# The remainder of a weight unit in the second expert product: one VectorE instruction of 1024 columns in place of two of 512

## The chip, the cores and the metric

One core of a Trainium2 chip runs the whole layer as one program. The metric is device time in microseconds (us), from the start to the end of the program; the median of the runs counts.

## What is computed

The reference is one layer of a diffusion backbone on 256 latent tokens of width 2048: modulated norm, two kinds of attention, an output projection, a second norm, and then product-key experts. Only the last part matters here. Each token picks 16 experts for each of 8 heads out of 16384, and what it adds is a weighted sum of rows of the table `v` (16384 x 2048):

```
act = jax.nn.gelu(jnp.einsum('cd,ced->ce', hc, u[ic]))
wts = (gc * act.astype(jnp.float32)).astype(v.dtype)
return jnp.einsum('ce,ced->cd', wts, v[ic])
```

The kernel computes these products densely for most tokens. For the first product all of `u` is streamed from HBM and multiplied with the activations, and for the second all of `v` is streamed and multiplied with a matrix that holds each token's weight for each expert (zero where it was not picked). The last 64 tokens of the second product are done otherwise: their rows of `v` are gathered by indirect DMA and added up on VectorE. All products are made to nearly fp32 accuracy out of fp32r operands: a value is split into a high part (fp32r) and a remainder (the value less its high part), and the cross products are summed.

## The kernel before

The change lies in the second expert product, the last 580 us or so of the program. The table `v` comes in 256 units of 128 partitions x 1024 fp32 columns (512 KB). Two units are one tile of 128 experts (all 2048 columns), and four units, two tiles, are one block; the value blocks have the numbers 98 to 161. What happens to a unit, in order:

- SyncE's DMA queue (`unit`, L301; later `unit_far`, L413, and `unit_near`, L418) loads it into a slot of a ring in SBUF. Up to block 110 there is one ring of four slots, `raw`; from block 111 on there are two of four, `raw_far` and `raw`, which blocks use in turn. A load into a slot is issued once the remainder of the unit that lay there has been made: it waits for the counter `w_low`, which counts halves.
- ScalarE (`half_high`, L566) rounds it to fp32r, half by half of 512 columns, into `w_hi`. This buffer holds four halves, so a half is rounded once TensorE has done with the half four before it (counter `w_free`). It counts up `w_high` after each half.
- VectorE (`half_low`, L1441, called twice by `split_low`) makes the remainder, unit less `w_hi`, into `w_lo`, which holds four halves too. It waits for `w_high` and counts up `w_low`.
- TensorE (`value_block`, L1378 to L1383) makes five products of 512 columns with a half: three with `w_hi` (L1378, L1379, L1380), for which it waits for `w_high`, and then two with `w_lo` (L1382, L1383), for which it waits for `w_low`. Then it counts up `w_free`.

A tile also has the stationary operand `p_hl`, the weights of the tokens for its 128 experts: ScalarE writes the high part (L870, L871), VectorE the remainder (`p_low`, L2041, 192 columns), and TensorE waits for both at the first of a tile's four halves. `p_hl` has two slots, so ScalarE writes the operand of a tile after TensorE has finished the tile two before.

Instructions of an engine run in program order. VectorE's order is that of `value_turn`: two units (the second tile of a block), `p_low` of the tile that follows, two units (the first tile of the next block), `p_low`. From the fourth turn on each tile also has an `add_half` (L2065, the first two L2072) ahead of `p_low`: 1024 columns of the gathered rows `row_t`, times the weight, are added to `mixed`. In 8 of the 60 turns that have them one more `add_half`, `early`, stands between the first two units. GpSimd fetches the rows of one gather (two indirect DMAs, L526, 128 partitions x 4 KB each) once a slot of `row_t` has been added. Four small `weights` (L2109) and two more stand at the starts of some turns.

Of the kernel before, what the change touches and what calls it, by code (L numbers as in the profile page):

```python
# [21 lines left out]
F32 = mybir.dt.float32  # L22
# [3 lines left out]
ALU = mybir.AluOpType  # L26
# [20 lines left out]
RAW, SPLIT, ADA, ADA1 = 4, 4, 4, 8  # L47
# [49 lines left out]
def block_program(nc, x_lat, x_ctx, par, con, w_ada, stream, sk, x2_dram, out):  # L97
    with ExitStack() as ctx:
# [10 lines left out]
        S = {n: ctx.enter_context(nc.semaphore(n)) for n in sem_names}  # L109
# [13 lines left out]
        def at(name, shape, dt, offset):  # L123
            return nc.alloc_sbuf_tensor_at(name, shape, dt, offset=base + offset)

        raw = at("raw", [P, RAW, UNIT], F32, 0)
        w_hi = at("w_hi", [P, SPLIT, HALF], F32R, 16 * KB)
        w_lo = at("w_lo", [P, SPLIT, HALF], F32R, 24 * KB)
# [101 lines left out]
        early = at("early", [P, 1], F32, R + 160 * KB)  # L230
# [1196 lines left out]
        def _(dve):  # L1427
            V_ = nc.vector
# [8 lines left out]
            def half_low(b, h, ring=raw):  # L1437

                dve.wait_ge(S["w_high"], 8 * b + (h + 1))
                at_ = (h % 2) * HALF  # L1440
                V_.tensor_tensor(w_lo[:, h % SPLIT, :], ring[:, h // 2 % RAW, at_:at_ + HALF],  # L1441
                                 w_hi[:, h % SPLIT, :].bitcast(F32), ALU.subtract).then_inc(S["w_low"], 1)

            def split_low(b, j, ring=raw):
                half_low(b, 2 * j, ring)
                half_low(b, 2 * j + 1, ring)
# [485 lines left out]
            low, high = slice(0, PICKED), slice(PICKED, P)  # L1932
# [84 lines left out]
            b0 = 34 + LATE_ADA_AT  # L2017
# [21 lines left out]
            def p_low(i, s):  # L2039
                dve.wait_ge(S["p_high"], i + 1)  # L2040
                V_.tensor_tensor(p_hl[:, s, DENSE:2 * DENSE], A[:, bass.ds(i, 1), 0:DENSE].rearrange("p a t -> p (a t)"),  # L2041
                                 p_hl[:, s, 0:DENSE].bitcast(F32), ALU.subtract).then_inc(S["p_low"], 1)
# [16 lines left out]
            def mix(r, s, hf):  # L2059

                cols = slice(hf * UNIT, (hf + 1) * UNIT)
                if hf == 0:
                    dve.wait_ge(row_in[s], 32 * r + 32)
                dve.wait_ge(S["mixed"], 8 * r + (2 * s + hf + 1))
                V_.scalar_tensor_tensor(mixed[:, cols], row_t[:, s, cols], weight[:, bass.ds(4 * r + s, 1)],  # L2065
                                        mixed[:, cols], ALU.mult, ALU.add).then_inc(S["mixed"], 1)

            def first_mix(hf):

                cols = slice(hf * UNIT, (hf + 1) * UNIT)  # L2070
                dve.wait_ge(row_in[0], 32)
                V_.tensor_scalar(mixed[:, cols], row_t[:, 0, cols], weight[:, 0:1], None, ALU.mult  # L2072
                                 ).then_inc(S["mixed"], 3 - 2 * hf)

            def ring_of(b):

                return raw_far if b >= FAR_AT and (b - FAR_AT) % 2 == 0 else raw

            def value_turn(b, b0, add=None, early=None):

                split_low(b + (98 + b0), 2, ring_of(98 + b0))
                if early is not None:
                    early()
                split_low(b + (98 + b0), 3, ring_of(98 + b0))
                if add is not None:
                    add(0)
                p_low(2 * b + (2 * b0 + 2), 0)
                split_low(b + (99 + b0), 0, ring_of(99 + b0))
                split_low(b + (99 + b0), 1, ring_of(99 + b0))
                if add is not None:  # L2090
                    add(1)
                p_low(2 * b + (2 * b0 + 3), 1)

            p_low(1, 1)
            gate_tiles(10, 3)
# [1 line left out]
            V_.tensor_tensor(fold[:], ident[:, 0:PICKED], ident[:, PICKED:P], ALU.add)  # L2097
            V_.tensor_scalar(row_far[:], row_near.bitcast(U32), P, None, ALU.add).then_inc(S["far_ready"], 1)
            for b in range(3):
                value_turn(0, b)  # L2100

            dve.wait_ge(S["values_kept"], 32)
            dve.wait_ge(S["p_high_too"], 8)
# [2 lines left out]
            def weights(g):  # L2106
                js = slice(([0] + PICK_ENDS)[g], PICK_ENDS[g])
                dve.wait_ge(pick_in[g], 16 * (js.stop - js.start))
                link(V_.tensor_tensor(weight[:, js], picked[:, js], gate_at[:, js], ALU.mult))  # L2109

            def add_half(n):

                if n < 2:
                    first_mix(n)
                else:
                    mix(n // 8, n // 2 % ROWS, n % 2)

            for g in range(4):
                n = 32 * g
                for b in range(15):  # L2120
                    if b in ((0, 3, 7) if g == 0 else (0,)):
                        weights(g + 2 if g else (b + 1) // 4)
                    three_halves = b in (3, 11)
                    m = n + three_halves
                    value_turn(0, 3 + 15 * g + b, lambda hf: add_half(m + hf), (lambda: add_half(n)) if three_halves else None)
                    n = m + 2
            split_low(161, 2, ring_of(161))
            split_low(161, 3, ring_of(161))

            dve.wait_ge(S["x2_in"], 16)  # L2130

# [155 lines left out]
```

## Time and profile before

| what | value |
|---|---|
| runs | 2033.44, 2037.87, 2039.68 us; median 2037.87 |
| the profiled execution | 2038.55 us; its span 2036.8 us, 1.75 us lie around it |
| TensorE's granted clock | 0.996 of full speed over the span |
| second expert product, first to last product | 1430.8 to 2014.2 us of the span |

The span runs from the first instruction to the last. Rows of a timeline give the start, the length, the engine, the line and the tile; a number behind x says how many instructions are merged, and what stands in brackets is how long the engine sat idle before and what ended it. A matmul shows as 0.39 us, of which the next one overlaps a part.

### The profile page before, as it was taken

To read this page: it belongs to the slowest core of one execution; us is meant where nothing else is said; L and a number is where in the kernel's file an instruction comes from. 1 tells how busy PE (TensorE), PEld (TensorE's weight loads), DVE (VectorE), ACT (ScalarE), POOL (GpSimd) and SP (SyncE) were. 2 spreads that over 40 slices of the span, in tenths; PEclk is the share of its full clock that TensorE was granted. 3 is DMA by queue.
4 is the path that set the end of the run, shared out by engine and by line. 5 is a ranking of instruction groups with operands and counts; after the bars stand their busy time and mean duration, and the time that the engine had idled before them with its cause. 6 is when DMAs were issued, how large, how long until landed. Compare 5 with 4: busy or idle time off the path is not lost.

```text
span 2036.8 us, 35895 instructions
## 1 busy us (share of the span) xinstructions
PE 2002.3 (98%) x10973; PEld 1681.6 (83%) x10973; DVE 1614.8 (79%) x2873; ACT 1117.9 (55%) x2232; POOL 604.2 (30%) x476
## 2 busy tenths in 40 slices
PE   7999999999999999999999999999999999999997
PEld 4578888767999988888888888888878888888886
DVE  4468787897778789899977655676789989989997
ACT  3342225586455555565565555555656666666666
POOL 0000000000000000018888887522455454323320
PEclk9999999999999999999999999999999999999999
DMA  9978887860777655658789887788999999999992
GB/s 387 404 270 295 297 272 288 259 185 2 260 278 273 232 182 179 193 181 192 188 238 282 229 214 189 224 284 284 335 347 379 364 354 356 352 353 367 385 356 97
DMA packets 217706, 550.28 MB, mean 270 GB/s; under 512 B 63888, under 2 KB 89376, under 8 KB 216992
## 3 DMA queue, kind: packets, MB, share of 16 engines
q1 hardware_dynamic: 148688, 465.21, 63.8%
q0 software_dynamic: 52512, 80.00, 15.0%
q10 hardware_dynamic: 16432, 4.19, 1.0%
q8 instruction: 33, 0.54, 0.1%
q14 instruction: 41, 0.34, 0.0%
HBM read 528.11 MB, written 21.07 MB: 270 GB/s over the span
## 4 chain that ended last, share of the span: by engine, by line
PE 90%; DVE 4%; DMA 3%; ACT 1%; issue 1%; DVEq 0%; SPq 0%; ACTq 0%
PE PS L977 23%; PE PS L1338 22%; PE PS L1343 11%; PE PS L1378 6%; PE PS L1383 5%; PE PS L1379 5%; PE PS L1382 5%; PE PS L1380 5%; DMA gt<-grid_scratch 2%; PE PS L1047 1%; DVE st L1649 1%; PE PS L1180 1%; PE PS L964 1%; DMA ada_t<-w_ada 1%; DVE w_lo L1441 1%
## 5 line engine op out<-in xcount | busy, mean ns | idle before, releaser
L566 ACT ACTIVATE w_hi<-raw 128x512 fp32r<-128x512 f32 x1088 | 681.5, 631 | 665.4 <-PE PS L977 255.5
L1441 DVE TENSOR_TENSOR w_lo<-raw,w_hi 128x512 fp32r<-128x512 f32 x1088 | 729.2, 689 | 245.1 <-ACT w_hi L566 211.2
L1338 PE MATMUL PS<-h,w_hi 128*128 128x512 f32 x2048 | 560.4, 395 | 0.0
L1338 PEld LDWEIGHTS PS<-h,w_hi 128*128 128x128 f32 x2048 | 350.7, 189 | 47.1
L1343 PEld LDWEIGHTS PS<-h,w_lo 128*128 128x128 f32 x2048 | 314.3, 189 | 47.9 <-DVE w_lo L1441 4.5
L1343 PE MATMUL PS<-h,w_lo 128*128 128x256 f32 x2048 | 326.7, 281 | 2.7 <-DVE w_lo L1441 2.6
L526 POOL DMA_INDIRECT row_t<-stream,i1T x128 | 163.6, 1278 | 299.2 <-DVE mixed L2065 253.9
L1378 PE MATMUL PS<-w_hi,p_hl 128*128 128x512 f32 x512 | 200.1, 391 | 1.1 <-ACT w_hi L566 0.6
L1382 PE MATMUL PS<-w_lo,p_hl 128*128 128x512 f32 x512 | 199.3, 389 | 0.0
L1379 PE MATMUL PS<-w_hi,p_hl 128*128 128x512 f32 x512 | 199.3, 389 | 0.0
L1380 PE MATMUL PS<-w_hi,p_hl 128*128 128x512 f32 x512 | 199.2, 389 | 0.0
L1383 PE MATMUL PS<-w_lo,p_hl 128*128 128x512 f32 x512 | 199.2, 389 | 0.0
L450 POOL MEMSET acc<- 128x1024 f32 x8 | 7.6, 955 | 595.8 <-PE PS L987 271.3
L566 ACT ACTIVATE w_hi<-raw_far 128x512 fp32r<-128x512 f32 x208 | 131.4, 633 | 82.4 <-PE PS L1383 72.5
L2065 DVE SCALAR_TENSOR_TENSOR mixed<-row_t,gT,mixed 128x1024 f32<-128x1024 f32 x126 | 161.6, 1282 | 0.0
L1441 DVE TENSOR_TENSOR w_lo<-raw_far,w_hi 128x512 fp32r<-128x512 f32 x208 | 137.8, 688 | 20.4 <-ACT w_hi L566 18.2
L1378 PEld LDWEIGHTS PS<-w_hi,p_hl 128*128 128x128 f32 x512 | 96.1, 188 | 24.1 <-issue 2.1
L456 POOL DMA_INDIRECT grid_scratch<-gate_b,addr_b x64 | 110.1, 1720 | 19.5 <-issue 19.5
L977 PE MATMUL PS<-w_hi,hl_h 128*128 128x512 f32 x288 | 113.9, 396 | 1.2 <-DVE w_lo L1441 1.2
L1382 PEld LDWEIGHTS PS<-w_lo,p_hl 128*128 128x128 f32 x512 | 96.1, 188 | 20.6 <-issue 0.4
L1380 PEld LDWEIGHTS PS<-w_hi,p_hl 128*128 128x128 f32 x512 | 96.1, 188 | 20.1
L1383 PEld LDWEIGHTS PS<-w_lo,p_hl 128*128 128x128 f32 x512 | 96.1, 188 | 19.8
(274 smaller groups left out, 3177.7 us busy)
## 6 DMA issues: line engine op xcount, KB each, us to landing
raw<-stream SPq DMA_DIRECT2D x544, 512.0 KB
ada<-w_ada SPq DMA_DIRECT2D x112, 512.0 KB
raw_far<-stream SPq DMA_DIRECT2D x104, 512.0 KB
ada_t<-w_ada SPq DMA_DIRECT2D x64, 512.0 KB, 7.9
grid_scratch<-zeros SPq DMA_DIRECT2D x8, 1536.0 KB, 14.1
gt<-grid_scratch POOLq DMA_DIRECT2D x64, 192.0 KB, 4.6
ada_u<-w_ada SPq DMA_DIRECT2D x16, 512.0 KB
values_scratch<-A ACTq DMA_DIRECT2D x1, 2560.0 KB
```

The costliest lines, as they stand in the source:

```text
L526: nc.gpsimd.indirect_dma_start(row_t[:, j % ROWS, hf * UNIT:(hf + 1) * UNIT], None, rows, bass.IndirectOffsetOnAxis(ap=index[:, j:j + 1], ...
L566: nc.scalar.activation(w_hi[:, (2 * j + hf) % SPLIT, :], ring[:, j, hf * HALF:(hf + 1) * HALF], ACT.Copy).then_inc(S["w_high"], 1)
L977: ins = mm(out_, l_, r_, start=(start and q == 0), stop=(stop and q == 2), skip_group_check=check)
L1338: mm(PS[:, i, :], w_hi[:, h % SPLIT, q * P:(q + 1) * P], h2[:, :, k, :], start=(k == 0), stop=False, skip_group_check=True)
L1343: ins = mm(PS[:, i, 0:T], w_lo[:, h % SPLIT, q * P:(q + 1) * P], h2_h[:, k, :], start=False, stop=(k == KT - 1), skip_group_check=True)
L1378: mm(near_, high, w_hi[:, h % SPLIT, :], start=begin, stop=False, skip_group_check=True)
L1379: mm(near_, low, w_hi[:, h % SPLIT, :], start=False, stop=False, skip_group_check=True)
L1380: mm(far_, both, w_hi[:, h % SPLIT, :], start=begin, stop=False, skip_group_check=True)
L1382: mm(near_, high, w_lo[:, h % SPLIT, :], start=False, stop=end, skip_group_check=True)
L1383: ins = mm(far_, both, w_lo[:, h % SPLIT, :], start=False, stop=end, skip_group_check=True)
L1441: V_.tensor_tensor(w_lo[:, h % SPLIT, :], ring[:, h // 2 % RAW, at_:at_ + HALF], w_hi[:, h % SPLIT, :].bitcast(F32), ALU.subtract).then_in ...
L2065: V_.scalar_tensor_tensor(mixed[:, cols], row_t[:, s, cols], weight[:, bass.ds(4 * r + s, 1)], mixed[:, cols], ALU.mult, ALU.add).then_inc ...
```

## The change

In the value turns VectorE makes the remainder of a whole unit with one instruction of 1024 columns in place of two of 512. A unit's two halves lie side by side in `w_lo` and in `w_hi`. The new `unit_low` waits until both halves of `w_high` are there, and counts up `w_low` by two at its end. `value_turn` loses a parameter that was always 0. All that comes before the second expert product's first two units, and the other engines' code, stay as they were.

```
-            def value_turn(b, b0, add=None, early=None):
-
-                split_low(b + (98 + b0), 2, ring_of(98 + b0))
+            def unit_low(b, j):
+
+                dve.wait_ge(S["w_high"], 8 * b + 2 * j + 2)
+                low, high = (a[:, 2 * j % SPLIT:2 * j % SPLIT + 2, :].rearrange("p a t -> p (a t)") for a in (w_lo, w_hi))
+                V_.tensor_tensor(low, ring_of(b)[:, j, :], high.bitcast(F32), ALU.subtract).then_inc(S["w_low"], 2)
+
+            def value_turn(b0, add=None, early=None):
+
+                unit_low(98 + b0, 2)
                 if early is not None:
                     early()
-                split_low(b + (98 + b0), 3, ring_of(98 + b0))
+                unit_low(98 + b0, 3)
                 if add is not None:
                     add(0)
-                p_low(2 * b + (2 * b0 + 2), 0)
-                split_low(b + (99 + b0), 0, ring_of(99 + b0))
-                split_low(b + (99 + b0), 1, ring_of(99 + b0))
+                p_low(2 * b0 + 2, 0)
+                unit_low(99 + b0, 0)
+                unit_low(99 + b0, 1)
...
-            split_low(161, 2, ring_of(161))
-            split_low(161, 3, ring_of(161))
+            unit_low(161, 2)
+            unit_low(161, 3)
```

On VectorE the first turn with three additions (the seventh value turn) stands so before; `w_lo<-raw,w_hi` is the remainder of halves, `mixed<-...` an `add_half`, `p_hl<-...` the remainder of a tile's operand, `gT<-...` the `weights`:

```order
L2109 TENSOR_TENSOR gT<-i2T,gT 128x4
L1441 TENSOR_TENSOR w_lo<-raw,w_hi 128x512 x2
L2065 SCALAR_TENSOR_TENSOR mixed<-row_t,gT,mixed 128x1024
L1441 TENSOR_TENSOR w_lo<-raw,w_hi 128x512 x2
L2065 SCALAR_TENSOR_TENSOR mixed<-row_t,gT,mixed 128x1024
L2041 TENSOR_TENSOR p_hl<-A,p_hl 128x192
```

and so after the change:

```order
L2115 TENSOR_TENSOR gT<-i2T,gT 128x4
L2083 TENSOR_TENSOR w_lo<-raw,w_hi 128x1024
L2065 SCALAR_TENSOR_TENSOR mixed<-row_t,gT,mixed 128x1024
L2083 TENSOR_TENSOR w_lo<-raw,w_hi 128x1024
L2065 SCALAR_TENSOR_TENSOR mixed<-row_t,gT,mixed 128x1024
L2041 TENSOR_TENSOR p_hl<-A,p_hl 128x192
```

Each pair has become one instruction; nothing has moved past anything. The same holds on VectorE where the additions begin, the fourth and fifth value turns, shown here with the waits, before:

```order
L2109 TENSOR_TENSOR gT<-i2T,gT 128x4 [waits p_low,pick_in0,p_high_too,values_kept]
L1441 TENSOR_TENSOR w_lo<-raw,w_hi 128x512 [waits w_high,dve]
L1441 TENSOR_TENSOR w_lo<-raw,w_hi 128x512 [waits w_high] x3
```

and after:

```order
L2115 TENSOR_TENSOR gT<-i2T,gT 128x4 [waits p_low,pick_in0,p_high_too,values_kept]
L2083 TENSOR_TENSOR w_lo<-raw,w_hi 128x1024 [waits w_high,dve]
L2083 TENSOR_TENSOR w_lo<-raw,w_hi 128x1024 [waits w_high]
L2072 TENSOR_SCALAR mixed<-row_t,gT 128x1024 [waits row_in0]
L2041 TENSOR_TENSOR p_hl<-A,p_hl 128x192 [waits p_high]
```

Four waits for `w_high` have become two, each for a half later than the first of its pair was. TensorE's, ScalarE's and SyncE's instructions are the same in the two kernels.

## Rows read from the trace of the kernel before

**Rows 1.** The page: busy time, DMA share in 40 slices, last chain

```profile
PE 2002.3 (98%) x10973; PEld 1681.6 (83%) x10973; DVE 1614.8 (79%) x2873; ACT 1117.9 (55%) x2232; POOL 604.2 (30%) x476
...
DMA  9978887860777655658789887788999999999992
...
PE 90%; DVE 4%; DMA 3%; ACT 1%; issue 1%; DVEq 0%; SPq 0%; ACTq 0%
```

**Rows 2.** One line's instructions (L1378): count, durations, first and last start

```profile
L1378 PE MATMUL PS<-w_hi,p_hl x512: 389/389/504, 1430.8 to 2013.3; 128*128 128x512 f32 x171
```

**Rows 3.** Waits of TensorE, 1425 to 2014 us: in total, times, longest

```profile
PE PS L1378 <- ACT w_hi L566: 0.6, 1, 0.6
PE PS L1378 <- DVE p_hl L2041: 0.4, 2, 0.2
```

**Rows 4.** Groups by line, 1450 to 2010 us: busy us, mean ns, idle before

```profile
L1441 DVE TENSOR_TENSOR w_lo<-raw,w_hi 128x512 fp32r<-128x512 f32 x285 | 187.7, 688 | 39.3 <-ACT w_hi L566 28.4 <-issue 8.8
...
L566 ACT ACTIVATE w_hi<-raw 128x512 fp32r<-128x512 f32 x284 | 177.2, 631 | 121.5 <-PE PS L1383 92.3 <-DMA raw<-stream 14.7 <-issue 8.7
L2065 DVE SCALAR_TENSOR_TENSOR mixed<-row_t,gT,mixed 128x1024 f32<-128x1024 f32 x126 | 161.6, 1282 | 0.0
...
L2041 DVE TENSOR_TENSOR p_hl<-A,p_hl 128x192 fp32r<-128x192 f32 x123 | 43.2, 352 | 0.0
```

**Rows 5.** Timeline of a tile in the steady part, three engines

```profile
1803.85 0.63 ACT L566 ACTIVATE w_hi<-raw_far 128x512 fp32r<-128x512 f32 x1 [0.50 <-PE PS L1383]
...
1804.32 2.02 DVE L1441 TENSOR_TENSOR w_lo<-raw_far,w_hi 128x512 fp32r<-128x512 f32 x3
...
1805.91 0.39 PE L1378 MATMUL PS<-w_hi,p_hl 128*128 128x512 f32 x1
...
1806.11 0.63 ACT L566 ACTIVATE w_hi<-raw_far 128x512 fp32r<-128x512 f32 x1 [0.50 <-PE PS L1383]
...
1806.78 0.69 DVE L1441 TENSOR_TENSOR w_lo<-raw_far,w_hi 128x512 fp32r<-128x512 f32 x1 [0.44 <-ACT w_hi L566]
...
1807.39 1.28 DVE L2065 SCALAR_TENSOR_TENSOR mixed<-row_t,gT,mixed 128x1024 f32<-128x1024 f32 x1
...
1808.58 0.35 DVE L2041 TENSOR_TENSOR p_hl<-A,p_hl 128x192 fp32r<-128x192 f32 x1
...
1810.45 0.39 PE L1378 MATMUL PS<-w_hi,p_hl 128*128 128x512 f32 x1
```

**Rows 6.** Timeline of VectorE in a turn with three additions

```profile
1836.05 1.28 DVE L1441 TENSOR_TENSOR w_lo<-raw,w_hi 128x512 fp32r<-128x512 f32 x2
1837.26 1.28 DVE L2065 SCALAR_TENSOR_TENSOR mixed<-row_t,gT,mixed 128x1024 f32<-128x1024 f32 x1
1838.45 1.29 DVE L1441 TENSOR_TENSOR w_lo<-raw,w_hi 128x512 fp32r<-128x512 f32 x2
```

**Rows 7.** Timeline around TensorE's longest stall, ring of four slots

```profile
1532.27 1.15 ACT L566 ACTIVATE w_hi<-raw 128x512 fp32r<-128x512 f32 x2 [2.49 <-PE PS L1383]
...
1532.93 1.30 DVE L1441 TENSOR_TENSOR w_lo<-raw,w_hi 128x512 fp32r<-128x512 f32 x2 [1.28 <-ACT w_hi L566]
...
1533.14 0.47 PE L1378 MATMUL PS<-w_hi,p_hl 128*128 128x512 f32 x1 [0.59 <-ACT w_hi L566]
...
1533.91 0.39 PE L1382 MATMUL PS<-w_lo,p_hl 128*128 128x512 f32 x1
```

**Rows 8.** Timeline of a lap of the ring of four slots

```profile
1503.90 2.57 DVE L1441 TENSOR_TENSOR w_lo<-raw,w_hi 128x512 fp32r<-128x512 f32 x4
...
1512.65 1.15 ACT L566 ACTIVATE w_hi<-raw 128x512 fp32r<-128x512 f32 x2 [2.68 <-DMA raw<-stream]
...
1513.31 1.30 DVE L1441 TENSOR_TENSOR w_lo<-raw,w_hi 128x512 fp32r<-128x512 f32 x2 [1.50 <-ACT w_hi L566]
```

**Rows 9.** Stages: length, busy (x count) of PE, PEld, DVE, ACT, POOL, clock, DMA, GB/s

```profile
1500.00:1550.00 50.00, 49.04 (x212) 39.08 (x211) 43.39 (x67) 30.33 (x66) 21.57 (x21) 1.00 0.94 343
1550.00:1600.00 50.00, 50.00 (x222) 41.41 (x221) 45.80 (x69) 32.23 (x66) 27.40 (x25) 1.00 1.03 400
```

More of the change, by code:

```diff
@@ L2077, in ring_of @@
                 return raw_far if b >= FAR_AT and (b - FAR_AT) % 2 == 0 else raw
-            def value_turn(b, b0, add=None, early=None):
-                split_low(b + (98 + b0), 2, ring_of(98 + b0))
+            def unit_low(b, j):
[4 more added lines that the diff above has]
+                unit_low(98 + b0, 2)
                 if early is not None:
                     early()
-                split_low(b + (98 + b0), 3, ring_of(98 + b0))
+                unit_low(98 + b0, 3)
                 if add is not None:
                     add(0)
-                p_low(2 * b + (2 * b0 + 2), 0)
-                split_low(b + (99 + b0), 0, ring_of(99 + b0))
-                split_low(b + (99 + b0), 1, ring_of(99 + b0))
+                p_low(2 * b0 + 2, 0)
+                unit_low(99 + b0, 0)
+                unit_low(99 + b0, 1)
                 if add is not None:
                     add(1)
-                p_low(2 * b + (2 * b0 + 3), 1)
+                p_low(2 * b0 + 3, 1)
             p_low(1, 1)
@@ L2099, in _ @@
             for b in range(3):
-                value_turn(0, b)
+                value_turn(b)
             dve.wait_ge(S["values_kept"], 32)
@@ L2124, in _ @@
                     m = n + three_halves
-                    value_turn(0, 3 + 15 * g + b, lambda hf: add_half(m + hf), (lambda: add_half(n)) if three_halves else None)
+                    value_turn(3 + 15 * g + b, lambda hf: add_half(m + hf), (lambda: add_half(n)) if three_halves else None)
                     n = m + 2
-            split_low(161, 2, ring_of(161))
-            split_low(161, 3, ring_of(161))
+            unit_low(161, 2)
+            unit_low(161, 3)
             dve.wait_ge(S["x2_in"], 16)
```

## The prediction

> **What bounds the kernel now.** I first read the page's busy times and its last chain [rows 1]: TensorE is busy for 98% of the span and makes 90% of the chain; VectorE is busy for 79% and makes 4%. So VectorE's time counts only where TensorE waits for it. The first product with `value` units starts at 1430.8 us and the last half starts at 2013.3 [rows 2], 582.5 us for 511 steps from half to half. In the steady part two tiles' first products start 1805.91 and 1810.45 [rows 5]: 4.54 us for four halves, 1.133 to 1.135 a half, or 0.2267 a product. 511 such steps are 579.0 to 580.0 us. All stalls of TensorE together are then 2.5 to 3.5 us of 2037; the waits that the trace names come to 1.0 [rows 3]. That is the most that any gain on VectorE can give back.
>
> They lie where the DMA is late. From 1500 to 1550 TensorE started 212 products in 50 us, afterwards 222 [rows 9]: ten products, 2.3 us, are lost there, while the ring still has four slots. The DMA share is 0.94 at 343 GB/s then, and 1.03 at 400 once the second ring fills. ScalarE waits 14.7 us for `raw` in all [rows 4].
>
> **What is removed and added.** 254 units (blocks 98 to 161, less the first two units) lose one VectorE instruction each. A half costs 688 ns, and 192 columns cost 352 [rows 4]: 336 ns for 320 columns, 1.05 ns a column. So 1024 columns are 688 + 512 x 1.05 = 1226 ns. Bounds: 1282 ns, the row of the other operation of 1024 columns, and 1075, 1024 columns at 1.05 with nothing fixed [rows 4]. I take 1.22 us, since that comes from the same operation. A following instruction starts some 0.07 us before the end shown (1836.05 + 1.28 against 1837.26) [rows 6], so a unit holds VectorE for 1.15 us where a pair held it for 1.21: 0.06 us less each, 15 us in 254. All of it lies under TensorE's products. Costed at nothing as a gain; it would be worth up to 15 us only if TensorE waited for VectorE throughout.
>
> The Trainium skill (VectorE: DVE Perf Modes, on the TRN2 errata) says that a fixed latency is paid for each instruction that reads SBUF, so that one large tile pays it once, and gives (N+151)/0.96 ns for an fp32 `tensor_tensor`. By that page a unit would be 1224 ns as an estimate, and the change a plain gain of 157 ns for each unit; the durations in this trace agree, but the starts in it show that back to back half of this was hidden already.
>
> **What is moved: steady part.** The wait for `w_high` comes one half later. ScalarE's four halves of one tile start 1.13 apart; the second starts at 1803.85 and the fourth at 1806.11 [rows 5], since each waits for TensorE to free its slot. Call the units of a tile A and B.
> - Before: A0's remainder starts at 1804.32, is done at 1805.01. TensorE begins the tile at 1805.91 and needs it three products later, at 1806.59: 1.6 us early. B1's starts at 1806.78, when its high part is done, then `add_half` at 1807.39, `p_low` at 1808.58 [rows 5].
> - After: B waits for B1's high part and starts at 1806.78, done at 1808.00; B0 is needed at 1805.91 + 2.27 + 0.68 = 1808.86, 0.86 early. `add_half` 1807.93, `p_low` 1809.12 to 1809.47, needed at 1810.45: 0.98 early. The next A starts at 1809.39 (its second high part has been there since 1809.01), done at 1810.61, needed at 1811.13: 0.5 early.
> - With three additions [rows 6] A is followed by another 1.19 us: B 0.42 after its high part, `p_low` 0.55 early, the next A 0.1 early; the B after that waits for ScalarE again, and the pattern is restored. With 1282 ns for a unit this last margin is nothing, about 0.1 us for each of 8 turns.
>
> So the steady part costs nothing; the cover is TensorE's buffer of four halves, and its smallest margin shrinks from about 1 us (`p_low` in such a turn) to 0.1.
>
> **What is moved: the ring of four.** Here units come late and ScalarE makes both halves at once when one lands. At TensorE's longest stall it starts at 1532.27 and has both done at 1533.42; VectorE starts at 1532.93, TensorE at 1533.14, and needs the first remainder at 1533.91; it was done at 1533.62 [rows 7]. After, VectorE starts at 1533.46 and is done at 1534.68: TensorE stands for another 0.77 us, 0.9 with the 0.1 that a restart costs in the same row (1533.14 to 1533.91 is 0.77 for three products). This delay is paid once, not at each late unit: a TensorE that is 0.9 us later finds the next late unit that much readier. The term is **+0.9**.
>
> Second, the slot comes free later. A unit lands at 1512.65, and its remainder was done 1.96 us later (1514.61) [rows 8]; after, it is 1.15 + 0.04 + 1.22 = 2.41: 0.45 later. The load four units on is issued that much later. The unit that landed at 1512.65 had been issued at about 1505.2, half way through the four remainders that start at 1503.90 [rows 8]: 7.5 us to land. 7.5 + 1.96 = 9.4 us is a lap, and TensorE uses four units in 9.07. So in this stage the lap is the bound at times. A lap is a turn, and of the 12 turns on the single ring 9 have additions and gathers. If landing takes as long as before, each of these laps is 0.45 later, +4.1. If the late landing is only the queue (share 0.94), a later issue lands at the same time: +0. Nearest to the rows is the second, since the DMA engines were nearly full; I take three tenths, **+1.2**.
>
> The Trainium skill (DMA: Bandwidth & Descriptors, on the anatomy of one DMA) gives 2.0 us + bytes/436 GB/s: as an estimate 3.2 us for such a unit, so that a lap would have over 3 us to spare and this second term would be nothing. The landing of 7.5 us speaks against it for a queue with other loads in it.
>
> **Sum.** 0 + 0.9 + 1.2 = 2.1 us, 2038.55 + 2.1 = 2040.6 for an execution like the profiled one. That lies 0.7 above the median of its runs, so the median should be 2037.87 + 2.1 = **2040.0**. The runs before spread from 2033.44 to 2039.68, so about 0.3% (6 us) is what can be told from no change.
>
> **Rivals.**
> - *No change in the measurement, +0.9 to +5.0 (my forecast).* Chance 0.80. It takes in both ends of the ring's term, 0.9 + 0 to 0.9 + 4.1; its own range is 2036 to 2043.
> - *The ring of four is bound by its lap throughout.* Slower by over 6 us. All 12 laps, each 0.51 later (0.45, and 0.06 more with the bound of 1282 ns for a unit), are 6.1; with the 0.9, 0.96 by that bound, 7.1: 2045. It decides where a unit takes over 9.07 - 1.96 = 7.1 us to land whatever the load. For it: 7.5 in [rows 8]. Against: with laps of 9.4 and more throughout, TensorE would have lost over 0.3 us in each of 12 before, over 4 us, and all its stalls are 2.5 to 3.5. Chance 0.13.
> - *VectorE was the late one, and is relieved.* TensorE waits for `p_low` twice, 0.4 us [rows 3], and `p_low` stands behind remainders. If all stalls were of that kind, -2.5 to -3.5: 2035. That is the most, and is still within 0.3%. For over 6 us TensorE would have to take its products faster than 0.2267 us, for which no row speaks. The skill's page on VectorE, whose rule makes fewer and larger instructions a gain, would point here. Chance of over 0.3%: 0.07, nearly all of it the scatter of the runs.
> - *The margins of 0.1 us do not hold.* 8 turns and late units in the far ring, each up to 0.9: +1 to +4, no other sign than the forecast's, and held in it.
>
> **Numbers.** Faster 0.07, within 0.3% 0.80, slower 0.13. Range: from 2034.5 (all stalls gone) to 2045.5 (the lap throughout).
>
> **What the profile of the changed kernel would show.** `w_lo` of 128x1024 at 1.22 us, 254 times. In the steady part VectorE idle 0.6 to 0.7 us ahead of B, TensorE at 222 products in 50 us, no wait. In the stage of the single ring TensorE waiting for `w_lo` at L1382, which it does nowhere before, in sum 1 to 4 us, and fewer than 212 products from 1500 to 1550. Wrong would be: TensorE waiting for `w_lo` in the steady part (margins misread), or a unit that takes 1.3 us or more; or a stage shorter than 582 us, which would mean that the stalls were VectorE's.

## The result

The changed kernel takes 2042.75 us (median of 9 runs, 2040.10 to 2045.94); the kernel before took 2036.63 in nine runs beside them (2032.80 to 2039.89). The ratio is 1.0026, with a 95% interval of 1.0014 to 1.0038: slower by 0.26%, 5 to 6 us, where +2.1 was forecast. The time lies inside the range, and 0.26% lies inside the likeliest case (no change beyond 0.3%), though the interval reaches past it. The size of the loss is two and a half to three times the forecast: its interval is +2.9 to +7.7 us, clear of zero and of +2.1. It lies above +5.0, where the forecast's own case ended. That 2042.75 is still within that case's 2036 to 2043 is luck: those bounds were set from the three runs of before with the median 2037.87, and the nine have 2036.63.

### The profile page after: what moved, and what is told of

Same layout as the page of the kernel before. It is cut to its first block and busy times, and to the rows that moved or that the text cites. A ratio compares the mean times of both kernels' runs of the same rounds, so it can differ in the third digit from the quotient of the medians.

```text
span 2038.6 us, 35889 instructions
## 1 busy us (share of the span) xinstructions
PE 2002.5 (98%) x10973; PEld 1678.9 (82%) x10973; DVE 1589.4 (78%) x2619; ACT 1119.9 (55%) x2232; POOL 649.3 (32%) x476
## 5 line engine op out<-in xcount | busy, mean ns | idle before, releaser
L1441 DVE TENSOR_TENSOR w_lo<-raw,w_hi 128x512 fp32r<-128x512 f32 x788 | 531.4, 689 | 206.2 <-ACT w_hi L566 195.3
L526 POOL DMA_INDIRECT row_t<-stream,i1T x128 | 208.1, 1626 | 252.2 <-DVE mixed L2065 211.7
L2083 DVE TENSOR_TENSOR w_lo<-raw,w_hi 128x1024 fp32r<-128x1024 f32 x150 | 183.1, 1221 | 60.0 <-ACT w_hi L566 58.6
L1382 PE MATMUL PS<-w_lo,p_hl 128*128 128x512 f32 x512 | 201.5, 394 | 1.9 <-DVE w_lo L2083 1.6
L1378 PE MATMUL PS<-w_hi,p_hl 128*128 128x512 f32 x512 | 199.4, 390 | 0.3 <-issue 0.3
L2083 DVE TENSOR_TENSOR w_lo<-raw_far,w_hi 128x1024 fp32r<-128x1024 f32 x104 | 126.9, 1220 | 33.4 <-ACT w_hi L566 33.3
L1382 PEld LDWEIGHTS PS<-w_lo,p_hl 128*128 128x128 f32 x512 | 96.1, 188 | 28.8 <-DVE w_lo L2083 9.1
L1378 PEld LDWEIGHTS PS<-w_hi,p_hl 128*128 128x128 f32 x512 | 96.1, 188 | 20.6 <-issue 0.4
L1380 PEld LDWEIGHTS PS<-w_hi,p_hl 128*128 128x128 f32 x512 | 96.1, 188 | 20.2
L1379 PEld LDWEIGHTS PS<-w_hi,p_hl 128*128 128x128 f32 x512 | 96.1, 188 | 20.1
```

The costliest lines, as they stand in the source:

```text
L526: nc.gpsimd.indirect_dma_start(row_t[:, j % ROWS, hf * UNIT:(hf + 1) * UNIT], None, rows, bass.IndirectOffsetOnAxis(ap=index[:, j:j + 1], ...
L1378: mm(near_, high, w_hi[:, h % SPLIT, :], start=begin, stop=False, skip_group_check=True)
L1379: mm(near_, low, w_hi[:, h % SPLIT, :], start=False, stop=False, skip_group_check=True)
L1380: mm(far_, both, w_hi[:, h % SPLIT, :], start=begin, stop=False, skip_group_check=True)
L1382: mm(near_, high, w_lo[:, h % SPLIT, :], start=False, stop=end, skip_group_check=True)
L2083: V_.tensor_tensor(low, ring_of(b)[:, j, :], high.bitcast(F32), ALU.subtract).then_inc(S["w_low"], 2)
```

## The profile after

The profiled execution took 2040.43 us, one of the quicker of the nine. Of the page, the busy times, which answer to [rows 1]:

```profile
PE 2002.5 (98%) x10973; PEld 1678.9 (82%) x10973; DVE 1589.4 (78%) x2619; ACT 1119.9 (55%) x2232; POOL 649.3 (32%) x476
```

VectorE has 254 instructions less and is busy for 25 us less; TensorE's work is the same. GpSimd is busy for 45 us more, with the same 476 instructions, which nobody had forecast. The groups by line from 1450 to 2010 us show both:

```profile
L526 POOL DMA_INDIRECT row_t<-stream,i1T x124 | 204.0, 1645 | 243.5 <-DVE mixed L2065 211.7 <-issue 23.3 <-PE PS L1383 6.5
...
L2083 DVE TENSOR_TENSOR w_lo<-raw,w_hi 128x1024 fp32r<-128x1024 f32 x143 | 174.5, 1221 | 53.7 <-ACT w_hi L566 52.3 <-issue 0.4
...
L2083 DVE TENSOR_TENSOR w_lo<-raw_far,w_hi 128x1024 fp32r<-128x1024 f32 x102 | 124.5, 1220 | 32.7 <-ACT w_hi L566 32.6
```

A unit costs VectorE 1.22 us, as reckoned from two widths. The last expert product, by its first line's first and last start (as [rows 2]):

```profile
L1378 PE MATMUL PS<-w_hi,p_hl x512: 389/389/468, 1429.1 to 2015.2; 128*128 128x512 f32 x171
```

From the first half to the last it is now 586.1 us, and was 582.5. Since 511 halves take 579.0 to 580.0 us without any stall, this one number shows TensorE's stalls in the stage, also those too short to be named as waits. I call it the stage's length below. What TensorE and ScalarE wait for from 1425 to 2014 us (as [rows 3]):

```profile
PE PS L1382 <- DVE w_lo L2083: 1.6, 3, 0.8
...
ACT w_hi L566 <- DMA raw<-stream: 24.4, 21, 2.2
```

TensorE now waits at L1382 for `w_lo`, which [rows 3] has nowhere. ScalarE's wait for the DMA was 15.8 us in that window before; in the second profiles of the two kernels, below, it is 19.9 with the change and 19.4 without, so it doesn't tell them apart. By stages (as [rows 9]):

```profile
1450.00:1500.00 50.00, 49.70 (x216) 39.77 (x216) 38.43 (x44) 30.14 (x63) 30.19 (x23) 1.00 0.95 339
1500.00:1550.00 50.00, 48.47 (x208) 38.29 (x207) 40.55 (x43) 29.37 (x64) 24.11 (x21) 1.00 0.95 346
1550.00:1600.00 50.00, 50.00 (x222) 41.11 (x221) 43.02 (x46) 32.27 (x66) 33.90 (x24) 1.00 1.01 380
```

The products in 50 us (the count behind PE) fall to 216 where they were 221 and to 208 where they were 212, and are 222 as before once the second ring is there. The steady part, as [rows 5]:

```profile
1807.19 0.63 ACT L566 ACTIVATE w_hi<-raw_far 128x512 fp32r<-128x512 f32 x1 [0.50 <-PE PS L1383]
...
1807.93 1.23 DVE L2083 TENSOR_TENSOR w_lo<-raw_far,w_hi 128x1024 fp32r<-128x1024 f32 x1 [0.71 <-ACT w_hi L566]
1809.07 1.28 DVE L2065 SCALAR_TENSOR_TENSOR mixed<-row_t,gT,mixed 128x1024 f32<-128x1024 f32 x1
1810.27 0.35 DVE L2041 TENSOR_TENSOR p_hl<-A,p_hl 128x192 fp32r<-128x192 f32 x1
1810.54 1.22 DVE L2083 TENSOR_TENSOR w_lo<-raw_far,w_hi 128x1024 fp32r<-128x1024 f32 x1
...
1811.53 0.39 PE L1378 MATMUL PS<-w_hi,p_hl 128*128 128x512 f32 x1
```

VectorE waits 0.71 us for the second high half of B, and the next A starts 2.61 us after B, as worked out. A is done at 1811.76 and needed at 1812.21, three products after 1811.53: 0.45 us early, where 0.5 was forecast. In a turn with three additions (as [rows 6]) nothing is left of the margin:

```profile
1842.67 1.22 DVE L2083 TENSOR_TENSOR w_lo<-raw_far,w_hi 128x1024 fp32r<-128x1024 f32 x1
...
1843.71 0.39 PE L1380 MATMUL PS<-w_hi,p_hl 128*128 128x512 f32 x1
1843.94 0.50 PE L1382 MATMUL PS<-w_lo,p_hl 128*128 128x512 f32 x1
1844.28 0.40 PE L1383 MATMUL PS<-w_lo,p_hl 128*128 128x512 f32 x1
```

The remainder is done at 1843.89, the product that needs it starts at 1843.94, and the next one comes 0.34 us later, not 0.23: 0.11 lost, as at TensorE's other restarts in this profile. Seven of the 8 such turns lie behind the single ring, and each loses 0.13 to 0.21 us there. One more turn, one of those that begin with `weights`, loses 0.36: its A comes 0.2 us too late. The waits from 1560 to 2014 us show all eight, at TensorE's weight loads:

```profile
PEld PS L1382 <- DVE w_lo L2083: 2.4, 8, 0.5
```

A weight load runs ahead of its product, so only a part of these 2.4 us is lost; from the products' starts it is 1.5 us.

In the single ring, a unit that ScalarE had waited for (as [rows 8]):

```profile
1443.72 1.15 ACT L566 ACTIVATE w_hi<-raw 128x512 fp32r<-128x512 f32 x2 [1.46 <-DMA raw<-stream]
...
1444.97 1.23 DVE L2083 TENSOR_TENSOR w_lo<-raw,w_hi 128x1024 fp32r<-128x1024 f32 x1 [1.39 <-ACT w_hi L566]
```

VectorE starts 1.25 us after ScalarE and is done after 2.48; before it was 0.66 and 1.96. So the slot comes free 0.52 us later, and the first half's remainder 1.1 us later (before, 1.35 after ScalarE's start).

## Experiments

All times are set against the kernel before, run in turn with them on the same chip (medians 2037.5 to 2037.7 there); 0.1% is 2.04 us. "Stage" is the length defined above, from each kernel's one profile.

The two columns on the right say how much TensorE lost in the stage: up to block 110, the single ring's blocks, and behind it. They are worked out from the same starts, less 1.1333 us for each half, which is the step where nothing is lost.

| kernel | ratio | 95% interval | stage, us | lost to 110 | lost after |
|---|---|---|---|---|---|
| before | 1 | | 582.5 | 2.7 | 0.7 |
| the change | 1.0026 | 1.0014 to 1.0038 | 586.1 | 5.4 | 1.5 |
| two halves with the late wait | 1.0025 | 1.0013 to 1.0036 | 586.0 | 6.8 | 0.0 |
| change in the second ring only | 1.0001 | 0.9989 to 1.0014 | 580.8 | 0.5 | 1.1 |
| change in the single ring only | 1.0024 | 1.0011 to 1.0037 | 588.4 | 9.2 | 0.0 |
| the change again | 1.0029 | 1.0018 to 1.0041 | 588.7 | 8.0 | 1.5 |
| before, 20 turns on the single ring | 1.0009 | 0.9995 to 1.0023 | 582.4 | 1.7 | 1.5 |
| change, 20 turns on the single ring | 1.0060 | 1.0042 to 1.0077 | 590.7 | 5.2 | 6.4 |
| before, short gathers | 0.9996 | 0.9985 to 1.0007 | 579.5 | 0.3 | 0.0 |
| change, short gathers | 1.0012 | 0.9998 to 1.0025 | 583.3 | 2.7 | 1.5 |
| before, slot half a unit later | 1.0059 | 1.0038 to 1.0080 | 597.4 | 18.2 | 0.1 |
| before, products wait for a whole unit | 1.0009 | 0.9997 to 1.0021 | 580.4 | 1.3 | 0.0 |
| before, operand ahead of the addition | 1.0004 | 0.9992 to 1.0016 | 581.7 | 2.6 | 0.0 |
| before again | 0.9996 | 0.9983 to 1.0009 | 579.7 | 0.6 | 0.0 |

**The late wait without the wide instruction.** In `unit_low` of the changed kernel:

```
                 dve.wait_ge(S["w_high"], 8 * b + 2 * j + 2)
-                low, high = (a[:, 2 * j % SPLIT:2 * j % SPLIT + 2, :].rearrange("p a t -> p (a t)") for a in (w_lo, w_hi))
-                V_.tensor_tensor(low, ring_of(b)[:, j, :], high.bitcast(F32), ALU.subtract).then_inc(S["w_low"], 2)
+                half_low(b, 2 * j, ring_of(b))
+                half_low(b, 2 * j + 1, ring_of(b))
```

> VectorE waits for both high halves as in the change, but makes the remainder in two instructions of 512 columns. If the loss is the later start and the later slot (my theory), this kernel loses as much as the change or a little less, since the first half is done 0.5 us earlier than with one instruction and the second 0.07 later: +3 to +6 us against before. If the instruction of 1024 columns itself costs (it holds VectorE and what it shares with GpSimd, whose indirect DMAs went from a mean of 1278 to 1645 ns), this kernel is within 1.5 us of before and GpSimd's indirect DMAs stay near 1280 ns.

It loses what the change loses, 0.25%. GpSimd's gathers are back at their old length, in the groups by line of this kernel:

```profile
L526 POOL DMA_INDIRECT row_t<-stream,i1T x124 | 155.5, 1254 | 295.4 <-DVE mixed L2065 254.9 <-issue 26.4 <-PE PS L1383 9.7
```

So the loss is the wait for the second half and what follows from it. Neither the wide instruction nor the slower GpSimd has a part in it that the times can tell. The profiles do show one: with two halves nothing is lost behind the single ring, where the wide instruction loses 1.1 to 1.5 us at the tight turns, in every profile of a kernel that has it there.

**In which ring.** `unit_low` begins with one of these:

```
+                if b < FAR_AT:      # second ring only; b >= FAR_AT: single ring only
+                    split_low(b, j, ring_of(b))
+                    return
```

> The change from block 111 on only, where there are two rings; 512 columns and the old wait before. My theory: the loss lies in the single ring, and what is left here are the tight turns with three additions and a late unit now and then: +0.5 to +2 us. The rival, that the small margins of the steady part are what costs: +4 us or more.

> The change up to block 110 only, the single ring of four slots; from block 111 on the kernel before. My theory: +2 to +5 us, most of the loss, with TensorE waiting for w_lo at L1382 between 1434 and 1550 us. The rival of the steady part: under +1.5 us.

The second ring's stage has 204 of the 254 units and no loss that the times show (1.0001); the single ring has 50 and 0.24%. The rival of the steady part's small margins falls as the main cause: it is left with the 1.1 to 1.5 us. In the first of the two the gathers take 1628 ns each as in the change, and it costs nothing:

```profile
L526 POOL DMA_INDIRECT row_t<-stream,i1T x126 | 205.1, 1628 | 245.6 <-DVE mixed L2065 210.2 <-issue 23.2 <-PE PS L1383 9.8
```

**The change again, and the kernel before again.** No edit.

> The changed kernel once more, beside the three others on one chip: +6 us by its nine runs (+4 to +8). The second profile shows how much TensorE's stalls in the last 585 us vary: 7.0 us in the first profile against 3.4 before. If the loss of 6 us lies in them, a slower execution shows more of them, above all in the single ring; if it shows the same 7 us, the rest of the loss lies elsewhere.

> The kernel before once more, for a second profile of its last stage on the chip of these runs. The same time as before within 0.1%; the stage between 580.5 and 584.5 us, its stalls of 1.6 to 5.5 us nearly all between 1434 and 1550 us. A stage of 586 us or more would mean that the differences between single profiles of the two kernels are scatter.

Stages are 586.1 and 588.7 us with the change, 582.5 and 579.7 before. The second profile of before has hardly any stall, below the 580.5 that I expected at least, and that of the change more than its first. Single profiles of one kernel thus differ by 2.6 to 2.8 us. By means 587.4 against 581.1, the stage is 6.3 us longer, as much as the timed runs lose. From 1466 us, about where the additions begin, to 1550, first the change again and then before again:

```profile
1466.00:1550.00 84.00, 81.24 (x347) 63.93 (x345) 66.22 (x72) 48.33 (x103) 38.26 (x36) 1.00 0.93 330
```

```profile
1466.00:1550.00 84.00, 83.94 (x370) 69.07 (x369) 72.97 (x114) 51.60 (x110) 44.91 (x39) 1.00 0.97 356
```

23 products less in 84 us, at 0.2267 us each 5.2 us. The DMA engines moved less with the change (330 GB/s at a share of 0.93 against 356 at 0.97), so they were not at their limit. The two first profiles lie between, with 352 products and 362 there. The longest stall in the change's second profile:

```profile
1528.67 1.15 ACT L566 ACTIVATE w_hi<-raw 128x512 fp32r<-128x512 f32 x2 [2.23 <-DMA raw<-stream]
...
1530.20 0.39 PE L1380 MATMUL PS<-w_hi,p_hl 128*128 128x512 f32 x1
1531.57 0.50 PE L1382 MATMUL PS<-w_lo,p_hl 128*128 128x512 f32 x1 [0.98 <-DVE w_lo L2083]
```

ScalarE had been idle for 2.23 us when the unit came; TensorE has made the three products that need only the high half, and stands at the fourth, 1.37 us after the third.

**20 turns on the single ring.** `FAR_TURN = 20` in place of 12, in the kernel before and in the changed one.

> The kernel before with the second ring from value turn 20 on, not 12 (blocks 119 on): 20 laps on the single ring of four slots. Before shows 2.7 us of stalls in 12 laps. If the lap limits now and then: +1 to +4 us against before. If the stalls are chance events that come with the beginning of the gathers: 0 to +1.

> The changed kernel with the same 20 laps. My theory, now that it sits in the single ring: the loss of the change is paid lap by lap (5 to 6 us in 12 laps, of which 9 have gathers; here 17 have), so +9 to +13 us against before and +7 to +10 against the kernel before with 20 laps. If it is paid once, when the first late unit comes or the stage begins: the same +6 against its partner as with 12 laps.

Before, 8 laps more cost 1.9 us by medians (interval -1.0 to +4.7) and little in the stage: 582.4 us, where 12 turns have 582.5 and 579.7. With the old waits the lap nearly keeps up with TensorE. The change loses 8.4 us to its partner by medians (2047.87 against 2039.48), 8.3 by stages (590.7 against 582.4) and 10.4 by the ratios, instead of 5 to 6. In the eight laps more, blocks 111 to 118, TensorE loses 5.1 us with the change and 1.5 without. So the loss grows with the laps, by some 0.4 us for each, and is not paid once. It isn't confined to the laps with additions either: before the 33rd half there are none yet, and TensorE has lost 0.8 to 2.8 us by then in the six profiles with the change or the late wait in the single ring, and 0.1 to 0.4 in six without; the attempt below has 1.5.

**Short gathers.** After the fourth gather the indirect DMAs fetch 64 columns each, a sixteenth; the kernel leaves out the rest, so its sum for the last 64 tokens is wrong:

```
+                if j >= ROWS:
...
+                            row_t[:, j % ROWS, hf * UNIT:hf * UNIT + 64], None, short_rows,
```

> The kernel before, whose gathers after the fourth fetch 64 columns instead of 1024 for each indirect DMA (so the sum for the last 64 tokens is made of stale rows), with all instructions and waits in place: a third of the stage's DMA traffic is gone. If late landings under load make the stalls, they go: -2 to -4 us against before, no stall of TensorE between 1434 and 1550 us.

> The changed kernel with the same short gathers (stale rows for the last 64 tokens too). If the change costs through units that land late (my theory): within 1.5 us of the kernel before with short gathers, what is left being the turns with three additions. If it costs through the engines' own order, whatever the DMA does: +4 to +7 us against that partner.

The kernel before gains 0.04% (-3.1 to +1.4 us), less than expected: by the second profile of before there can be as little as 0.6 us to give back. The change stands 1.4 us above it by medians and 3.3 by ratios, whose intervals overlap. The times alone therefore don't settle whether the loss is gone. The profiles show where it went. First the kernel before with short gathers, then the change with them, from 1434 to 1466 us (before the additions, where the first four gathers are full ones), from 1466 to 1550, and in 100 us of the steady part:

```profile
1434.00:1466.00 32.00, 31.24 (x140) 25.78 (x139) 23.17 (x44) 20.29 (x45) 14.82 (x14) 1.00 0.94 327
1466.00:1550.00 84.00, 84.00 (x372) 69.34 (x371) 74.21 (x114) 53.34 (x111) 44.90 (x39) 1.00 0.82 264
...
1800.00:1900.00 100.00, 100.00 (x443) 82.81 (x442) 90.38 (x135) 64.69 (x134) 28.89 (x23) 1.00 0.82 260
```

```profile
1434.00:1466.00 32.00, 31.26 (x136) 25.04 (x135) 18.65 (x23) 18.87 (x40) 18.38 (x15) 1.00 0.92 324
1466.00:1550.00 84.00, 83.92 (x369) 68.61 (x368) 71.62 (x77) 53.86 (x112) 48.82 (x38) 1.00 0.82 264
...
1800.00:1900.00 100.00, 99.94 (x440) 82.27 (x440) 85.98 (x91) 64.52 (x132) 41.18 (x24) 1.00 0.77 258
```

Where the traffic was taken away the change now makes 369 products against 372, where it had made 347 to 352. By the starts of the halves, TensorE loses 0.7 us with short gathers between the 33rd half and block 110, where the change lost 4.6 and 5.9. Before that, where the traffic is as it was, it loses 2.0 us as in the other profiles; the two lines from 1434 us can't be set against each other, since the one stage starts at 1436.0 us and the other at 1427.2. In the steady part it loses the same 1.5 us at the tight turns. So the large part of the loss needs the DMA traffic of the gathers, which is to say units that land late; the tight turns do not.

**Which of the two delays.** The change makes the first half later for TensorE and the slot later for the DMA. Each was put alone into the kernel before. The slot, in SyncE's loop for blocks 98 to 110:

```
-                sp.wait_ge(S["w_low"], 8 * b + 2 * (j - 3))
+                sp.wait_ge(S["w_low"], 8 * b + 2 * (j - 3) + 1)
```

> The kernel before, but in the single ring of blocks 98 to 110 a load waits for one half more: the slot comes free 0.6 us later or more (with the first half of the next unit), and nothing else is late. If the later slot of the change (0.45 us a lap) is the main part of its loss of 6 us, this kernel loses about as much or more: +4 to +12 us against before, with TensorE waiting at L1378 for w_hi. If the later first half is the main part: +0 to +2 us, and the stage near its 582.5 us.

The first half, in `value_block`:

```
-                    pe.wait_ge(S["w_low"], 8 * b + (2 * U_V + h + 1))
+                    pe.wait_ge(S["w_low"], 8 * b + (2 * U_V + (h | 1) + 1))
```

> The kernel before, but TensorE waits with the fourth product of a unit's first half until both halves of w_lo are there; VectorE and the loads are as before. The first half comes 0.6 us later for TensorE (1.06 in the change), the slot no later of itself. If the later first half is the main part of the loss: +3 to +6 us. If it is paid once and the slot is the main part: +0 to +2 us.

The later slot costs 12 us (7.7 to 16.3), and TensorE waits for the high half, not for `w_lo`; in this kernel's waits L1382 is the first product of a half, the old L1378:

```profile
PE PS L1382 <- ACT w_hi L570: 9.1, 8, 1.7
...
ACT w_hi L570 <- DMA raw<-stream: 63.2, 37, 4.5
```

But the slot is late by more than the 0.6 us of one remainder, since the half that the load waits for belongs to a unit that is late itself. One such load, with the remainders of the unit that lay in the slot (first line) and of the next one (its first half is done at 1490.63):

```profile
1487.27 1.29 DVE L1445 TENSOR_TENSOR w_lo<-raw,w_hi 128x512 fp32r<-128x512 f32 x2 [1.52 <-ACT w_hi L570]
...
1489.95 2.53 DVE L1445 TENSOR_TENSOR w_lo<-raw,w_hi 128x512 fp32r<-128x512 f32 x4
...
1490.81 0.33 SPq L409 DMA_DIRECT2D raw<-stream  x1
```

The slot's remainders are done at 1488.56, and the load is issued 2.25 us later. Over the 48 loads of blocks 99 to 110 the mean is 2.22 us, and 0.17 or 0.18 in the profiles of before and of the change: 2.05 us later, four times what the change does to the slot. The cost, 1 us a lap by the times and 1.4 by the stage, is a half to two thirds of that delay.

TensorE's own wait for the whole unit costs 1.8 us (-0.6 to +4.3), with a stage of 580.4. So a later first half alone costs little. It was later by 0.6 us here and by 1.1 in the change. The kernel of two halves with the late wait can be set beside it: there the first half is late by much the same, 0.5 to 0.6 us, and the slot by 0.5 too. It loses 5.1 us, so the slot makes about 3.3 of them. That is barely clear of noise by the times alone (some 0 to 7 us), but TensorE loses 6.8 us in the single ring with both delays and 1.3 with the first half's alone.

Does a load that is issued later also land later? Where ScalarE waited for a unit of the single ring (14 to 21 units in a profile), it took a mean of 6.7 us from the load's issue to ScalarE's start in both profiles before, and 6.8 and 7.0 with the change: it was no shorter for being issued later. With the slot 2.05 us later it took 6.0, so there a part of the delay was made good.

**An attempt at a faster kernel.** In the kernel before, `p_low` moves ahead of `add_half` in each tile.

```
-                if add is not None:
-                    add(0)
                 p_low(2 * b + (2 * b0 + 2), 0)
+                if add is not None:
+                    add(0)
```

> The kernel before with p_low ahead of add_half in each tile, an attempt at a faster kernel: the operand comes 1.2 us earlier, and three of the stalls before (0.24, 0.37 and 0.35 us) were at a tile's first product with p_low just ahead. -1.5 to 0 us against before; the stage under 582.5 us. More than 1.5 us would mean that the operand was behind the other stalls too.

1.0004 (0.9992 to 1.0016): no gain. Probably the stalls at a tile's first product were there when the unit itself was late, and the operand was only the last of what was waited for; no run shows this by itself.

## Why the prediction held, and where its size was off

- *TensorE bounds the stage and VectorE's saved time is worth nothing.* Right: 25 us less on VectorE, no gain anywhere, and none in the second ring alone (1.0001). Of the kernel before it read one profile, with 2.5 to 3.5 us of stalls; the second has 0.6. A stage under 582 us is therefore no sign of relieved stalls, as the prediction had it.
- *The wide instruction takes 1226 ns from two widths.* 1221 measured.
- *The steady part costs nothing, with 0.5 us and 0.1 us as the smallest margins.* Right but for 1.1 to 1.5 us: the margins are 0.45 and 0.05, and each tight turn costs 0.13 to 0.21 for a restart. The prediction named TensorE waiting for `w_lo` there as a sign that the margins were misread, and it does wait. A turn with `weights` at its start was not worked out at all. The rival that the margins don't hold had this, at the low end of its +1 to +4. The change in the second ring alone is at +0.2 us (-2.2 to +2.9), so the times can't tell it from nothing.
- *"+0.9", paid once by TensorE at a late unit.* Such stalls are there (three named waits of 1.6 us in all in one profile). That the term itself is small agrees with the kernel in which the products wait for a whole unit, +1.8 (-0.6 to +4.3).
- *The ring's term, "I take three tenths, +1.2".* This is the term that was mis-sized. The ends that I gave it were +0 and +4.1. The release was later by 0.52 us (0.45 reckoned), in all 12 turns and not only the 9 with additions, and 12 x 0.52 is 6.2 us. Measured are 4.9 us (2.2 to 7.5) for the change in the single ring alone, 0.4 for each lap, with what is left of the "+0.9" in it: most of the 0.52 came through. I chose the low end because the DMA engines' share was 0.94, as if a load had to queue whatever its issue. The loads that were issued later took as long as before, 6.8 and 7.0 us against 6.7, and so landed later. The kernel whose slot alone is 2.05 us later, and whose loads have the same queue before them, lost 1 us a lap: about half came through there.
- *The rival "bound by its lap throughout", 2045, chance 0.13.* Its mechanism was nearer to what happened than my term, at 0.4 us a lap. Its price of 7.1 us is inside the measured interval (2.9 to 7.7), where my 2.1 is not; that the case which I called likeliest came true owes much to the bound of 0.3%, which takes in 5.3 us. Its claim that the lap bound already before is wrong: 20 turns in place of 12 cost the kernel before 1.9 us (-1.0 to +4.7). My argument against it, that such laps would have shown over 4 us of stalls before, only showed that the lap was near balance then, and it says nothing of what comes on top.
- *The rival of the relieved VectorE.* Fell: nothing is faster.
- *The estimate of 3.2 us for a load.* The Trainium skill (DMA: Bandwidth & Descriptors, on the anatomy of one DMA) gives its formula for DMAs that GpSimd issues, and these are SyncE's. This case's loads take 6.7 us and more where ScalarE waits for them, with other loads and gathers in flight.

Open is how the loss of the change divides exactly between the later slot and the later first half. The runs speak for the slot as the larger part, about two thirds in the kernel with two halves.

## What to carry to other kernels

Where a buffer is released by the last step of a chain, count the time from the landing to the release as part of the ring's lap, and compare the lap with what the consumer takes for as many units. Near balance, most of what a merged instruction adds to that time can be paid in every lap (here 0.4 of 0.52 us), while the busy time it saves on an engine that does not bound is worth nothing. A high DMA share does not show that a later issue is hidden. A merged instruction saves a fixed cost, and pays for it with a wait for the later of its inputs.

## What was not expected of the hardware

GpSimd's indirect DMAs of rows (L526) take a mean of 1571 to 1702 ns in the five profiles whose steady part has remainders of 1024 columns, and 1218 to 1312 ns in the nine where it has 512, among them the one with the late wait. The short gathers are no shorter in either group (1702 and 1291 ns). So it is the width of VectorE's instruction, and not the wait, that holds GpSimd up. The Trainium skill (SBUF — State Buffer, in its terms) says that VectorE and GpSimd share a pair of ports that is held for a full instruction. By that rule a longer instruction holds GpSimd off longer, and the rows agree with it as far as that. The same page (Who interferes with whom) limits it, for a VectorE instruction with two inputs in SBUF as these are, to GpSimd instructions that read SBUF; no run here shows the port itself, or what of GpSimd's work waits. It cost no time: the kernel with the change in the second ring only has the long ones (1628 ns) and the time of before.
